# Another load order, blocks and a later root in the first steps of a two-block transformer kernel on one Trainium2 core

## Chip, core and metric

One core of a Trainium2 chip. The metric is the device time of one execution, in microseconds (us). The inputs and outputs are float32 in HBM; the kernel computes 256 tokens of width 2048 through two transformer blocks.

## What is computed

Only the beginning of the first block matters here. In the reference:

```python
h = rmsnorm(x, norm_attn[l])          # x: 256 x 2048
proj = h @ w_in[l]                    # 2048 x 6144, in q, k, v for heads A and heads B
qa = rope(qa.reshape(B, S, A_HEADS, HEAD_DIM), cos_a, sin_a)
ya = dilated_attention(qa, ka, va)
lam = exp(sum(lq[0] * lq[1])) - exp(sum(lq[2] * lq[3])) + lam_init
```

Behind it come a second kind of attention, an output projection and a gated FFN, then a second block with retention, block attention, gates and a convolved FFN, and a last norm. All of it is the same before and after the change.

## The kernel before, in words

**Steps.** All large products are cut into steps, one weight tile of 512 rows by 512 columns (1 MiB) each, numbered t = 0, 1, 2 and on. The three tiles of lead (LEAD) and a ring of four tiles (RING, `w_raw`) set how far the loads run ahead. A float32 product is made of three: ScalarE rounds a tile to `w_hi` (L1377), VectorE subtracts to get `w_lo` (L1906), and TensorE adds hi x hi, lo x hi and hi x lo. A step is 24 matmuls of 128x512: 2 token halves, 4 row blocks, 3 products (`products`, L834). While TensorE works at step t, ScalarE and VectorE run `split(t + LEAD)` and then `pieces(t)`, in program order.

**The transposed x.** `xt` (2048 x 256) comes from HBM in four quarters into `xt_raw`, ScalarE multiplies by the norm's gains into `xt_hi` (L1353), VectorE makes `xt_lo` (L1920). The norm's scale per token is applied later, when results are read from PSUM: for that x itself is loaded too, ScalarE squares and sums it (`square_sum`, L1404), VectorE makes the mean (`variance`), ScalarE takes the root (`root`), VectorE the reciprocal (`inverse`). Two exponentials for lam stand between.

**The first steps.** The first FIRST = 2 tiles are split by blocks of 128 rows; tile 0 is also loaded by blocks (`first_raw`). SyncE (SP) issues: tile 0 in four DMAs, xt quarter 1, tile 1, xt quarter 2, tile 2, xt quarter 3, tile 3, then half of x (two DMAs), tile 4, the other half of x, tile 5, tile 6 and on; from tile 4 it waits for `lo_ready` of the tile whose slot is taken, four before. ScalarE issues xt quarter 0, the gains and the identity. GpSimd issues both rope tables and lambda at once, and after the first step the two masks and the convolution taps. TensorE waits for the identity, does 14 transposes of it (L1160) to warm up, and goes into step 0 (L844 to L846), which waits block by block.

**Round 0** has 12 steps: 0 to 3 give q, 4 to 7 k, 8 to 11 v. What is done with the q of round 0, by program order on each engine:

- t = 0 and 1, ScalarE: the eight squares. t = 2: VectorE `variance(0)`, lambda sums, `inverse(0)`; ScalarE root and exponentials (`start`, L1590 and L2243).
- t = 3, ScalarE: `read_group` of q out of PSUM, scaled (L1582). t = 3, VectorE: rope on q (`rope_step`, L186; L2077 to L2080), which signals `stage_roped`.
- t = 6, TensorE: after the 24 matmuls of step 6 it waits for `stage_roped` and transposes q with eight transposes (`stage_turn`, L900; the step is in `turn_steps`, L178: `return ROUND_T[r] + 6, ROUND_T[r] + 9`), and only then goes on to step 7. t = 9: the same for k.
- t = 4, VectorE, after `pieces(4)`: `s_sums("rounds1")` (L1993 to L2000), sums of blocks of xt that later steps (from t = 12) use. t = 5, ScalarE: `s_hi_piece`.

VectorE's loop, which sets the order that the steps below follow:

```python
for t in range(FFN1_T):
    ...
    split(t + LEAD)
    if not softmax_step(t):
        pieces(t)
    if ROUNDS_1 and t == 4:
        s_sums("rounds1", 0, a_sum_early, sa_sum)
```

Softmax steps begin at t = 13 (L196), so in all steps of interest the split stands before the pieces.

Of the kernel before, what the change touches and what calls it, by code (L numbers as in the profile page):

```python
# [179 lines left out]
def rope_step(r, j):  # L180

    if r in UNIT_ROUNDS and KIND[r] != "R":
        return STEP[("round", r), ("U3" if r in P3_ROUNDS else "P7", "P4")[j]]
    if (r, j) == (4, 1):
        return STEP[("round", r), "P2"]
    return ROUND_T[r] + (5 if (r, j) == (5, 0) else 4 * j + 3)  # L186

# [24 lines left out]

WARM_UP = 14

FIRST = 2
DMA_SCRATCH = 1024
# [12 lines left out]
def plan_weights():  # L229
# [5 lines left out]
    count = [0] * RAW_SLOTS  # L235
    count[0] = -1

# [239 lines left out]
def build(nc, ins, out):  # L477
# [141 lines left out]
    x_loaded = [sem(f"x_loaded{q}") for q in range(Q)]  # L619
    xt_loaded = [sem(f"xt_loaded{q}") for q in range(Q)]  # L620
    first_raw = [sem(f"first_raw{j}") for j in range(C)]
    ident_loaded = sem("ident_loaded")
# [143 lines left out]
    @block.sync  # L766
    def _(sp):
        xr = ins["x"].rearrange("b (a p) d -> p (b a) d", p=P)
        def load_x(q):
            sp.dma_start(x[:, :, q * N:(q + 1) * N], xr[:, :, q * N:(q + 1) * N]).then_inc(x_loaded[q], 16)  # L770

        first = loads[0]
        for j in range(C):
            sp.dma_start(raw_tile(first.slot)[:, j], ins[first.weight][0][bass.ds(first.row + j * P, P), bass.ds(
                first.col, N)]).then_inc(first_raw[j], 16)
        for k, ld in enumerate(loads):
            if k == 0:
                continue
            if k < RING:
                sp.dma_start(xt_raw[:, C * k:C * (k + 1), :], ins["xt"][:, C * k:C * (k + 1), :]).then_inc(xt_loaded[k], 16)  # L780
            if k in (RING, RING + 1):
                load_x(2 * (k - RING))
                load_x(2 * (k - RING) + 1)
            if ld.made is not None:
                sp.wait_ge(sum_ready, sums[ld.made].count)
            elif ld.release >= 0:
                sp.wait_ge(lo_ready, ld.release + 1)
            sp.dma_start(raw_tile(ld.slot), tile_of(ins[ld.weight][0], ld.row, ld.col)).then_inc(
                raw_ready[ld.slot], 16)

        for tok in range(TOK):
            for q in (2, 3):
                cols = slice(q * N, (q + 1) * N)
                sp.wait_ge(out_dve_ready, 2 * tok + q - 1)
                sp.dma_start(orr[tok][:, cols], x[:, tok, cols]).then_inc(stored, 16)
        sp.wait_ge(stored, 16 * Q * TOK)

    @block.gpsimd
    def _(pool):
        def load(dst, src, signal):  # L800
            pool.dma_start(dst, src).then_inc(signal, 16)

        load(rope_a[:], ins["rope_a"], ropes_loaded)
        load(rope_b[:], ins["rope_b"], ropes_loaded)
        load(lq, ins["lambda_qk"].partition_broadcast(P)[:, 0], lam_loaded)
        pool.wait_ge(tile_used, 1)
        load(mask_a[:], ins["mask_a"], tables_loaded)
# [25 lines left out]
    def _(pe):  # L833
        def products(t, parts, first=True, last=True, shared=False, between=None, signal=tile_used):  # L834
# [4 lines left out]
            if t == 0:  # L839
                for j in range(C):  # L840
                    pe.wait_ge(xt_first_lo_done, j + 1)
                    pe.wait_ge(first_lo_ready, j + 1)
                    for bank, hi, lo in parts:
                        nc.tensor.matmul(bank, hi[:, j, :], w_hi[:, 0, j, :], start=j == 0, stop=False)  # L844
                        nc.tensor.matmul(bank, hi[:, j, :], w_lo[:, 0, j, :], start=False, stop=False)
                        end = nc.tensor.matmul(bank, lo[:, j, :], w_hi[:, 0, j, :], start=False, stop=False)  # L846
                end.then_inc(signal, 1)
                return
            for (bank, hi, lo), first in zip(parts, firsts):
                if between is not None and bank is parts[-1][0]:  # L850
# [306 lines left out]

        pe.wait_ge(ident_loaded, 16)
        for _ in range(WARM_UP):
            nc.tensor.transpose(acc[:, 0, 0, 0:P], ident[:, :], ident[:, :])  # L1160

# [188 lines left out]
    def _(act):  # L1350
        def xt_first_hi(c):
            act.wait_ge(xt_loaded[c // C], 16)
            copy(xt_hi[:, c, :], xt_raw[:, c, :], gains[:, G_ATTN1 + c:G_ATTN1 + c + 1]).then_inc(xt_first_hi_done, 1)  # L1353

        def split(t):
            if t >= STEPS:
                return
            if t == 0:
                for j in range(C):
# [3 lines left out]
                        first_hi_ready, 1)  # L1363
                return
            if t in sums:
                act.wait_ge(sum_ready, sums[t].count)
            else:
                act.wait_ge(raw_ready[steps[t].slot], steps[t].count)
            if t < FIRST:
                for j in range(C):  # L1370
                    nc.scalar.activation(w_hi[:, t, j], raw_tile(steps[t].slot)[:, j], ACT.Copy).then_inc(
                        first_hi_ready, 1)
                return
            if t >= RING:
                act.wait_ge(tile_used, t - RING + 1)
            rows = slice(0, 2) if t in sums and sums[t].name == "E5" else slice(0, C)
# [26 lines left out]

        def square_sum(zn, tok, q):  # L1404
            if squares[0]:
                act.wait_ge(sumsq_done, squares[0])
# [167 lines left out]
        def projections(t):  # L1574
            for r in range(8):
                rs = rstd[:, 0, :] if r < 4 else rstd[:, 3, :]
                plain = r not in UNIT_ROUNDS
                for j in range(2):
                    if (plain or KIND[r] == "R") and t == ROUND_T[r] + 4 * j + 3:
                        if 2 * r + j > 0:  # L1580
# [9 lines left out]
        def start(t):  # L1590
            if t in (0, 1):
                for q in (2 * t, 2 * t + 1):
                    act.wait_ge(x_loaded[q], 16)
                    for tok in range(TOK):
                        square_sum(0, tok, q)
            if t == 2:
                root(0)
# [18 lines left out]

        act.dma_start(xt_raw[:, 0:C, :], ins["xt"][:, 0:C, :]).then_inc(xt_loaded[0], 16)
        act.dma_start(gains[:, :], ins["gains"]).then_inc(gains_loaded, 16)
        act.dma_start(ident[:, :], ins["ident"]).then_inc(ident_loaded, 16)
        act.wait_ge(gains_loaded, 16)  # L1620
# [235 lines left out]
    def _(dve):  # L1856
# [29 lines left out]
        def split(t):  # L1886
# [3 lines left out]
            if t >= STEPS:  # L1890
                return
            if t not in sums:
                dve.wait_ge(raw_ready[steps[t].slot], steps[t].count)
            if t < FIRST:
                for j in range(C):
                    if t == 0:
                        xt_first_lo(j)
                    dve.wait_ge(first_hi_ready, C * t + j + 1)
                    nc.vector.tensor_tensor(w_lo[:, t, j], raw_tile(steps[t].slot)[:, j], w_hi[:, t, j].bitcast(F32),
# [343 lines left out]
        def start(t):  # L2243
            if t == 2:
                variance(0)
# [25 lines left out]
        def softmax_step(t):  # L2271
            return any(KIND[r] != "R" and attention_part(r, t) >= 0 for r in range(8))

        dve.wait_ge(gains_loaded, 16)
        for t in range(LEAD):
# [341 lines left out]
```

## Time and profile before

| what | before |
|---|---|
| device time, median of 3 runs | 2482.72 us (2482.7 to 2482.93) |
| time of the profiled execution | 2482.84 us |
| its span in the profile | 2481.0 us |
| TensorE busy | 2463.4 us (99%) |
| VectorE busy | 2105.0 us (85%) |
| ScalarE busy | 1518.1 us (61%) |
| first matmul of step 0 | 12.00 us after the span's start |

The span runs from the first to the last recorded event of the execution; the 1.8 us that the time has over it lie around it. Times of rows are microseconds from the span's start. Busy time of an engine is the union of its instructions.

### The profile page before, as it was taken

To read this page: it belongs to the slowest core of one execution; us is meant where nothing else is said; L and a number is where in the kernel's file an instruction comes from. 1 tells how busy PE (TensorE), PEld (TensorE's weight loads), DVE (VectorE), ACT (ScalarE), POOL (GpSimd) and SP (SyncE) were. 2 spreads that over 40 slices of the span, in tenths; PEclk is the share of its full clock that TensorE was granted. 3 is DMA by queue.
4 is the path that set the end of the run, shared out by engine and by line. 5 is a ranking of instruction groups with operands and counts; after the bars stand their busy time and mean duration, and the time that the engine had idled before them with its cause. 6 is when DMAs were issued, how large, how long until landed. Compare 5 with 4: busy or idle time off the path is not lost.

```text
span 2481.0 us, 28409 instructions
## 1 busy us (share of the span) xinstructions
PE 2463.4 (99%) x11260; PEld 2040.6 (82%) x11260; DVE 2105.0 (85%) x1717; ACT 1518.1 (61%) x1442; POOL 101.8 (4%) x95
## 2 busy tenths in 40 slices
PE   8999999999999999999999999999999999999998
PEld 7888888888888888888888888888888888888887
DVE  6878667899999999879688787877799999999997
ACT  6645555566666666665565565444566667766666
POOL 0000000000000000000000000000000000000000
PEclk9999999999999999999999999999999999999999
DMA  8546446677777777775455556557557777777775
GB/s 305 177 163 204 152 153 207 210 236 237 237 237 237 236 236 239 212 249 189 168 172 184 187 197 219 174 173 241 173 195 239 230 230 231 231 231 230 230 248 159
DMA packets 262580, 524.57 MB, mean 211 GB/s; under 512 B 9088, under 2 KB 9216, under 8 KB 262192
## 3 DMA queue, kind: packets, MB, share of 16 engines
q1 hardware_dynamic: 238688, 474.51, 55.9%
q0 software_dynamic: 22752, 46.55, 10.3%
q8 instruction: 90, 1.47, 0.2%
q10 hardware_dynamic: 1008, 1.68, 0.2%
q14 instruction: 42, 0.34, 0.0%
HBM read 478.67 MB, written 2.10 MB: 194 GB/s over the span
## 4 chain that ended last, share of the span: by engine, by line
PE 97%; DMA 1%; DVE 1%; ACT 0%; SPq 0%; issue 0%; ACTq 0%; DVEq 0%
PE acc L855 23%; PE acc L859 23%; PE acc L857 23%; PE misc L855 6%; PE misc L859 6%; PE misc L857 6%; PE acc L868 1%; PE acc L872 1%; PE acc L870 1%; PE misc L900 1%; DMA w_raw<-in_w_in 1%; PE misc L908 1%; PE misc L868 1%; PE misc L872 1%; PE misc L870 1%; PE misc L991 0%
## 5 line engine op out<-in xcount | busy, mean ns | idle before, releaser
L1906 DVE TENSOR_TENSOR w_lo<-w_raw,w_hi 128x2048 fp32r<-128x2048 f32 x475 | 1065.6, 2254 | 157.0 <-ACT w_hi L1377 155.6
L1377 ACT ACTIVATE w_hi<-w_raw 128x2048 fp32r<-128x2048 f32 x475 | 896.1, 1890 | 337.7 <-PE acc L859 234.5
L855 PE MATMUL acc<-w_hi,xt_hi 128*128 128x512 f32 x1132 | 447.1, 395 | 0.5 <-DVE w_lo L1906 0.4
L859 PE MATMUL acc<-w_hi,xt_lo 128*128 128x512 f32 x1132 | 441.3, 390 | 0.0
L857 PE MATMUL acc<-w_lo,xt_hi 128*128 128x512 f32 x1132 | 440.6, 389 | 0.0
L855 PEld LDWEIGHTS acc<-w_hi,xt_hi 128*128 128x128 f32 x1132 | 212.6, 188 | 45.0 <-issue 1.3
L859 PEld LDWEIGHTS acc<-w_hi,xt_lo 128*128 128x128 f32 x1132 | 212.4, 188 | 44.9
L857 PEld LDWEIGHTS acc<-w_lo,xt_hi 128*128 128x128 f32 x1132 | 212.7, 188 | 42.6
L1906 DVE TENSOR_TENSOR w_lo<-w_raw_more,w_hi 128x2048 fp32r<-128x2048 f32 (+1 forms) x99 | 222.2, 2244 | 29.8 <-ACT w_hi L1377 29.8
L1377 ACT ACTIVATE w_hi<-w_raw_more 128x2048 fp32r<-128x2048 f32 (+1 forms) x99 | 186.4, 1885 | 58.4 <-DVE w_raw_more L1877 15.8
L1881 DVE TENSOR_TENSOR w_raw<-w_raw 128x2048 f32<-128x2048 f32 x80 | 182.9, 2286 | 0.1
L855 PE MATMUL misc<-w_hi,xt_hi 128*128 128x512 f32 x452 | 178.7, 395 | 0.0
L859 PE MATMUL misc<-w_hi,xt_lo 128*128 128x512 f32 x452 | 176.3, 390 | 0.0
L857 PE MATMUL misc<-w_lo,xt_hi 128*128 128x512 f32 x452 | 176.0, 389 | 0.0
L1380 ACT ACTIVATE staged<-acc 128x1024 f32<-128x1024 f32 x80 | 82.4, 1030 | 116.0 <-PE acc L859 116.0
L855 PE MATMUL acc<-w_hi,h_hi 128*128 128x512 f32 x320 | 126.1, 394 | 0.0
L859 PE MATMUL acc<-w_hi,h_lo 128*128 128x512 f32 x320 | 124.9, 390 | 0.0
L857 PE MATMUL acc<-w_lo,h_hi 128*128 128x512 f32 x320 | 124.6, 389 | 0.0
L855 PE MATMUL acc<-w_hi,ht_hi 128*128 128x512 f32 x320 | 124.6, 389 | 0.0
L857 PE MATMUL acc<-w_lo,ht_hi 128*128 128x512 f32 x320 | 124.5, 389 | 0.0
L859 PE MATMUL acc<-w_hi,ht_lo 128*128 128x512 f32 x320 | 124.5, 389 | 0.0
L830 POOL DMA_DIRECT2D x<-staged x40 | 47.6, 1191 | 1290.1 <-ACT staged L1380 1276.0
(386 smaller groups left out, 4180.8 us busy)
## 6 DMA issues: line engine op xcount, KB each, us to landing
w_raw<-in_w_in SPq DMA_DIRECT2D x135, 1024.0 KB, 5.1
w_raw<-in_w_ffn_up SPq DMA_DIRECT2D x61, 1024.0 KB, 6.1
w_raw<-in_w_ffn_down SPq DMA_DIRECT2D x42, 1024.0 KB, 5.8
x<-staged POOLq DMA_DIRECT2D x80, 512.0 KB, 6.4
w_raw<-in_w_out SPq DMA_DIRECT2D x32, 1024.0 KB, 5.2
w_raw<-in_w_gate SPq DMA_DIRECT2D x32, 1024.0 KB, 6.6
w_raw<-in_w_down SPq DMA_DIRECT2D x32, 1024.0 KB, 7.0
w_raw<-in_w_up SPq DMA_DIRECT2D x27, 1024.0 KB, 5.2
```

The source lines that it names most:

```text
L830: pool.dma_start(x[:, :, n * N:(n + 1) * N], staged[k][:], accum_op=ALU.add).then_inc(staged_added[k], 16)
L855: nc.tensor.matmul(bank, hi[:, j, :], w_hi[:, t % RING, j, :], start=first and j == 0, stop=False, skip_group_check=shared)
L857: nc.tensor.matmul(bank, hi[:, j, :], w_lo[:, t % RING, j, :], start=False, stop=False, skip_group_check=shared)
L859: end = nc.tensor.matmul(bank, lo[:, j, :], w_hi[:, t % RING, j, :], start=False, stop=last and j == C - 1, skip_group_check=shared)
L868: nc.tensor.matmul(bank, hi[:, j, :], w_hi[:, t % RING, j0 + j, :], start=new and j == 0, stop=False, skip_group_check=True)
L870: nc.tensor.matmul(bank, hi[:, j, :], w_lo[:, t % RING, j0 + j, :], start=False, stop=False, skip_group_check=True)
L872: end = nc.tensor.matmul(bank, lo[:, j, :], w_hi[:, t % RING, j0 + j, :], start=False, stop=True, skip_group_check=True)
L900: end = nc.tensor.transpose(misc[:, banks[j // 2], (j % 2) * S + tok * P:(j % 2) * S + (tok + 1) * P], src[:, tok, j * P:(j + 1) * P], ide ...
L1377: nc.scalar.activation(w_hi[:, t % RING, rows], raw_tile(steps[t].slot)[:, rows], ACT.Copy).then_inc(hi_ready, 1)
L1380: return nc.scalar.activation(dst, src, func, scale=scale, **kw)
L1881: nc.vector.tensor_tensor(mine, other, mine, ALU.subtract).then_inc(sum_ready, 1)
L1906: nc.vector.tensor_tensor(w_lo[:, t % RING, rows], raw_tile(steps[t].slot)[:, rows], w_hi[:, t % RING, rows].bitcast(F32), ALU.subtract).t ...
```

## The change

In the order of the file:

- rope on the q of round 0 moves from t = 3 to t = 5 on VectorE, and the read of this q from PSUM from t = 3 to t = 5 on ScalarE. The transposition of q on TensorE stays at t = 6, `s_sums` at t = 4.
- 10 warm-up matmuls of 128x128 on a zeroed part of `junk` (a memset on VectorE) take the place of the 14 transposes of the identity. TensorE waits for the identity at step 4 instead.
- FIRST = RING = 4: tiles 0 to 3 are all loaded by blocks of 128 rows (16 DMAs of 256 KB), split by blocks and waited for by blocks.
- SP's order is now: gains, tile 0, xt quarter 1, tile 1, xt quarter 2, tile 2, xt quarter 3, tile 3, tile 4, tile 5, half of x, tile 6, the other half of x, tile 7 and on. ScalarE issues only xt quarter 0, as two halves.
- GpSimd issues the rope tables, lambda and the identity after step 0, the masks and taps after step 4.
- The squares move from t = 0, 1 to t = 3, 4, root, mean, reciprocal and lambda from t = 2 to t = 5.

```diff
-    return ROUND_T[r] + (5 if (r, j) == (5, 0) else 4 * j + 3)
+    return ROUND_T[r] + (5 if (r, j) in ((0, 0), (5, 0)) else 4 * j + 3)
...
-WARM_UP = 14
-
-FIRST = 2
+WARM_UP = 10
+
+FIRST = RING
...
-        first = loads[0]
-        for j in range(C):
-            sp.dma_start(raw_tile(first.slot)[:, j], ins[first.weight][0][bass.ds(first.row + j * P, P), bass.ds(
-                first.col, N)]).then_inc(first_raw[j], 16)
+        sp.dma_start(gains[:, :], ins["gains"]).then_inc(gains_loaded, 16)
         for k, ld in enumerate(loads):
-            if k == 0:
+            if k < FIRST:
+                if k:
+                    sp.dma_start(xt_raw[:, C * k:C * (k + 1), :], ins["xt"][:, C * k:C * (k + 1), :]).then_inc(
+                        xt_loaded[1 + k], 16)
+                for j in range(C):
+                    sp.dma_start(raw_tile(ld.slot)[:, j], ins[ld.weight][0][bass.ds(ld.row + j * P, P), bass.ds(
+                        ld.col, N)]).then_inc(first_raw[C * k + j], 16)
                 continue
...
-            if k in (RING, RING + 1):
-                load_x(2 * (k - RING))
-                load_x(2 * (k - RING) + 1)
+            if k in (RING + 2, RING + 3):
+                load_x(2 * (k - RING - 2))
+                load_x(2 * (k - RING - 2) + 1)
...
+        pool.wait_ge(tile_used, 1)
         load(rope_a[:], ins["rope_a"], ropes_loaded)
         load(rope_b[:], ins["rope_b"], ropes_loaded)
         load(lq, ins["lambda_qk"].partition_broadcast(P)[:, 0], lam_loaded)
-        pool.wait_ge(tile_used, 1)
+        load(ident[:, :], ins["ident"], ident_loaded)
+        pool.wait_ge(tile_used, 5)
         load(mask_a[:], ins["mask_a"], tables_loaded)
...
+            if t == 4:
+                pe.wait_ge(ident_loaded, 16)
...
-        pe.wait_ge(ident_loaded, 16)
+        pe.wait_ge(warm_ready, 1)
         for _ in range(WARM_UP):
-            nc.tensor.transpose(acc[:, 0, 0, 0:P], ident[:, :], ident[:, :])
+            nc.tensor.matmul(acc[:, 0, 0, 0:P], junk[:, 0:P], junk[:, 0:P], start=True, stop=True)
...
+            if t < FIRST:
+                for j in range(C):
+                    act.wait_ge(first_raw[C * t + j], 16)
+                    nc.scalar.activation(w_hi[:, t, j], raw_tile(steps[t].slot)[:, j], ACT.Copy).then_inc(
+                        first_hi_ready, 1)
+                return
...
-                    if (plain or KIND[r] == "R") and t == ROUND_T[r] + 4 * j + 3:
+                    if (plain or KIND[r] == "R") and t == ROUND_T[r] + 4 * j + (5 if (r, j) == (0, 0) else 3):
...
         def start(t):
-            if t in (0, 1):
-                for q in (2 * t, 2 * t + 1):
+            if t in (3, 4):
+                for q in (2 * t - 6, 2 * t - 5):
                     act.wait_ge(x_loaded[q], 16)
                     for tok in range(TOK):
                         square_sum(0, tok, q)
-            if t == 2:
+            if t == 5:
                 root(0)
...
-        act.dma_start(xt_raw[:, 0:C, :], ins["xt"][:, 0:C, :]).then_inc(xt_loaded[0], 16)
-        act.dma_start(gains[:, :], ins["gains"]).then_inc(gains_loaded, 16)
-        act.dma_start(ident[:, :], ins["ident"]).then_inc(ident_loaded, 16)
+        for half in range(2):
+            rows = slice(2 * half, 2 * half + 2)
+            act.dma_start(xt_raw[:, rows, :], ins["xt"][:, rows, :]).then_inc(xt_loaded[half], 16)
...
         def start(t):
-            if t == 2:
+            if t == 5:
                 variance(0)
...
+        nc.vector.memset(junk[:, 0:P], 0.0).then_inc(warm_ready, 1)
         dve.wait_ge(gains_loaded, 16)
```

## Rows read from the trace of the kernel before

**Rows 1.** Page, busy time by engine, and waits of TensorE over the whole span

```profile
PE 2463.4 (99%) x11260; PEld 2040.6 (82%) x11260; DVE 2105.0 (85%) x1717; ACT 1518.1 (61%) x1442; POOL 101.8 (4%) x95
...
PE acc L1160 <- DMA ident<-in_ident: 9.1, 1, 9.1
PE acc L855 <- DVE w_lo L1906: 0.4, 1, 0.4
```

**Rows 2.** Timeline of PE (start us, us): warm-up, steps 0, 1 and 6, transposition, step 7

```profile
9.10 3.25 PE L1160 MATMUL acc<-ident 128*128 128x128 f32 x14 [9.10 <-DMA ident<-in_ident]
12.00 0.78 PE L844 MATMUL acc<-w_hi,xt_hi 128*128 128x512 f32 x1
...
13.86 0.54 PE L845 MATMUL acc<-w_lo,xt_hi 128*128 128x512 f32 x1
14.23 0.40 PE L846 MATMUL acc<-w_hi,xt_lo 128*128 128x512 f32 x1
14.47 0.40 PE L844 MATMUL acc<-w_hi,xt_hi 128*128 128x512 f32 x1
...
18.58 0.39 PE L855 MATMUL acc<-w_hi,xt_hi 128*128 128x512 f32 x1
...
24.02 0.39 PE L855 MATMUL acc<-w_hi,xt_hi 128*128 128x512 f32 x1
...
46.33 0.50 PE L855 MATMUL acc<-w_hi,xt_hi 128*128 128x512 f32 x1 [0.39 <-DVE w_lo L1906]
...
51.93 1.03 PE L900 MATMUL misc<-ident,qk_stage 128*128 128x128 f32 x8
52.73 0.47 PE L855 MATMUL acc<-w_hi,xt_hi 128*128 128x512 f32 x1
```

**Rows 3.** DMA issues in 0 to 3 us: KB each, us to landing

```profile
y<-in_lambda_qk POOLq DMA_DIRECT2D x1, 128.0 KB, 7.7
rope_a<-in_rope_a POOLq DMA_DIRECT2D x1, 64.0 KB, 6.0
ident<-in_ident ACTq DMA_DIRECT2D x1, 64.0 KB, 7.4
...
rope_b<-in_rope_b POOLq DMA_DIRECT2D x1, 32.0 KB, 6.8
```

**Rows 4.** Tile w_raw, blocks 0 and 3 of tile 0 (windows 0.7:1.1, 2.1:2.3)

```profile
DMA to landing us min/median/max: 5.5/5.5/5.5
...
DMA to landing us min/median/max: 8.3/8.3/8.3
```

**Rows 5.** Timeline of ACT and DVE, first block of tile 0

```profile
8.29 0.61 ACT L1362 ACTIVATE w_hi<-w_raw 128x512 fp32r<-128x512 f32 x1
...
8.94 0.69 DVE L1899 TENSOR_TENSOR w_lo<-w_raw,w_hi 128x512 fp32r<-128x512 f32 x1
```

**Rows 6.** Tile w_raw, tile 7: issue on SP and landing (window 26.7:27)

```profile
L788 SPq DMA_DIRECT2D w_raw<-in_w_in x1: 2199/2199/2199, 26.8 to 26.8; - x1
...
DMA to landing us min/median/max: 14.3/14.3/14.3
```

**Rows 7.** Tile w_raw, tile 8: issue on SP and landing (window 34.0:34.3)

```profile
L788 SPq DMA_DIRECT2D w_raw<-in_w_in x1: 367/367/367, 34.0 to 34.0; - x1
...
DMA to landing us min/median/max: 9.7/9.7/9.7
```

**Rows 8.** DMA issues in 18.9 to 20.5 us: KB each, us to landing

```profile
mask_a<-in_mask_a POOLq DMA_DIRECT2D x1, 256.0 KB, 5.7
mult_a<-in_mult_a POOLq DMA_DIRECT2D x1, 256.0 KB, 6.3
taps<-in_taps POOLq DMA_DIRECT2D x1, 176.0 KB, 6.4
```

**Rows 9.** Timeline of ACT, 31 to 46 us: squares, split 5, root, exponentials, read of q

```profile
31.48 0.61 ACT L1407 ACTIVATE junk<-x 128x512 f32<-128x512 f32 x1
...
34.32 0.19 ACT L1407 ACTIVATION_READ_ACCUMULATOR junk<-x 128x1 f32 x1
...
35.71 1.92 ACT L1377 ACTIVATE w_hi<-w_raw 128x2048 fp32r<-128x2048 f32 x1 [1.20 <-DMA w_raw<-in_w_in]
...
41.85 0.20 ACT L1599 ACTIVATE lams<-lams 128x2 f32<-128x2 f32 x1
...
43.76 1.25 ACT L1380 ACTIVATE qk_stage<-acc,rstd 128x512 f32<-128x512 f32 x2
```

**Rows 10.** Timeline of DVE, 37 to 57 us: splits 5 to 8, rope on q, s_sums

```profile
37.73 2.29 DVE L1906 TENSOR_TENSOR w_lo<-w_raw,w_hi 128x2048 fp32r<-128x2048 f32 x1 [3.76 <-ACT w_hi L1377]
...
46.19 0.29 DVE L2077 TENSOR_TENSOR junk<-qk_stage,rope_a 128x128 f32<-128x128 f32 x1
...
47.18 0.43 DVE L2080 TENSOR_TENSOR qk_stage<-qk_stage,junk 128x256 f32<-128x256 f32 x1
47.52 2.28 DVE L1906 TENSOR_TENSOR w_lo<-w_raw,w_hi 128x2048 fp32r<-128x2048 f32 x1
49.72 2.29 DVE L1993 TENSOR_TENSOR a_sum_early<-xt_hi,xt_lo 128x2048 f32<-128x2048 f32 x1
...
54.70 2.28 DVE L1906 TENSOR_TENSOR w_lo<-w_raw,w_hi 128x2048 fp32r<-128x2048 f32 x1
```

**Rows 11.** Stretches (busy PE, PEld, DVE, ACT, POOL; PEclk; DMA; GB/s) and last matmul

```profile
12.00:13.80 1.80, 1.80 (x6) 1.47 (x5) 1.65 (x5) 1.45 (x4) 0.00 (x0) 1.00 1.06 420
...
2472.62 0.39 PE L859 MATMUL acc<-w_hi,h_last_lo 128*128 128x512 f32 x1
...
2473.10:2475.00 1.90, 0.00 (x0) 0.00 (x0) 1.55 (x4) 0.82 (x3) 0.00 (x0) 1.00 0.00 0
2475.00:2475.50 0.50, 0.00 (x0) 0.00 (x0) 0.32 (x2) 0.27 (x2) 0.00 (x0) 0.68 0.00 0
2475.50:2477.00 1.50, 0.00 (x0) 0.00 (x0) 0.99 (x2) 1.18 (x2) 0.00 (x0) 0.50 0.20 74
```

More of the change, by code:

```diff
@@ L235, in plan_weights @@
     count = [0] * RAW_SLOTS
-    count[0] = -1
+    for slot in range(RING):
+        count[slot] = -1
     def load(weight, row, col, release, slots=RING, last_sum=None):
@@ L619, in build @@
     x_loaded = [sem(f"x_loaded{q}") for q in range(Q)]
-    xt_loaded = [sem(f"xt_loaded{q}") for q in range(Q)]
-    first_raw = [sem(f"first_raw{j}") for j in range(C)]
+    xt_loaded = [sem(f"xt_loaded{c}") for c in range(2)] + [sem(f"xt_quarter_loaded{q}") for q in range(1, Q)]
+    first_raw = [sem(f"first_raw{j}") for j in range(C * FIRST)]
+    warm_ready = sem("warm_ready")
     ident_loaded = sem("ident_loaded")
@@ L770, in load_x @@
             sp.dma_start(x[:, :, q * N:(q + 1) * N], xr[:, :, q * N:(q + 1) * N]).then_inc(x_loaded[q], 16)
-        first = loads[0]
-        for j in range(C):
-            sp.dma_start(raw_tile(first.slot)[:, j], ins[first.weight][0][bass.ds(first.row + j * P, P), bass.ds(
-                first.col, N)]).then_inc(first_raw[j], 16)
+        sp.dma_start(gains[:, :], ins["gains"]).then_inc(gains_loaded, 16)
         for k, ld in enumerate(loads):
-            if k == 0:
-                continue
-            if k < RING:
-                sp.dma_start(xt_raw[:, C * k:C * (k + 1), :], ins["xt"][:, C * k:C * (k + 1), :]).then_inc(xt_loaded[k], 16)
-            if k in (RING, RING + 1):
-                load_x(2 * (k - RING))
-                load_x(2 * (k - RING) + 1)
+            if k < FIRST:
[5 more added lines that the diff above has]
+                        ld.col, N)]).then_inc(first_raw[C * k + j], 16)
+                continue
+            if k in (RING + 2, RING + 3):
+                load_x(2 * (k - RING - 2))
+                load_x(2 * (k - RING - 2) + 1)
             if ld.made is not None:
@@ L1351, in xt_first_hi @@
         def xt_first_hi(c):
-            act.wait_ge(xt_loaded[c // C], 16)
+            act.wait_ge(xt_loaded[c // 2 if c < C else 1 + c // C], 16)
             copy(xt_hi[:, c, :], xt_raw[:, c, :], gains[:, G_ATTN1 + c:G_ATTN1 + c + 1]).then_inc(xt_first_hi_done, 1)
@@ L1368, in split @@
                 act.wait_ge(raw_ready[steps[t].slot], steps[t].count)
[L1369 to L1375, printed above, removed]
+            act.wait_ge(tile_used, t - RING + 1)
             rows = slice(0, 2) if t in sums and sums[t].name == "E5" else slice(0, C)
@@ L1404, in square_sum @@
         def square_sum(zn, tok, q):
+            if not squares[0]:
+                act.wait_ge(tile_used, 1)
             if squares[0]:
@@ L1891, in split @@
                 return
-            if t not in sums:
+            if t not in sums and t >= FIRST:
                 dve.wait_ge(raw_ready[steps[t].slot], steps[t].count)
@@ L1897, in split @@
                         xt_first_lo(j)
+                    dve.wait_ge(first_raw[C * t + j], 16)
                     dve.wait_ge(first_hi_ready, C * t + j + 1)
```

## The prediction

> **What bounds the kernel now.** I read the page first: TensorE is busy 2463.4 of 2481.0 us, and in the list of its waits only two entries stand for the whole span, 9.1 us for the identity at the start and 0.4 us for a `w_lo` [rows 1]. So the time is the moment at which TensorE starts, plus its work, plus a short tail; whatever moves TensorE at the start moves the end by as much, if nothing gives it back. TensorE's timeline shows where that moment lies: the warm-up from 9.10, step 0 from 12.00, step 1's first matmul at 18.58 and step 2's at 24.02, so one step is 5.44 us (24 matmuls 0.227 us apart), step 6 from 46.33 after the 0.4 us wait, the transposes of q at 51.93, step 7 at 52.73 [rows 2]. No other step is late. Then I followed what the change moves onto TensorE's path, and there the decisive place is not step 0 but that transposition of q: TensorE doesn't go to step 7 before VectorE has roped q. Before, rope ends at 47.61 (47.18 + 0.43 [rows 10]) and TensorE comes at 51.93: 4.3 us to spare.
>
> **Part 1, the start: a gain of some 3.5 us up to the transposes.** Before, ScalarE's chain hangs on the gains, issued behind xt quarter 0, and its first `w_hi` starts at 8.29; a block then takes from the start of its `w_hi` at 8.29 to the end of its `w_lo` at 9.63, 1.34 us [rows 5], and TensorE could have begun near 9.7 but is in its warm-up until 12.00 [rows 2]. After, gains are first on SP and the warm-up needs no load, so step 0 hangs on the blocks. The last block of tile 0 lands before at 10.4 (issued near 2.1, 8.3 later), the first, issued at 0.7, at 0.7 + 5.5 = 6.2 [rows 4]. The tables taken out of the way (lambda, both ropes, identity: 288 KB, 0.28 MiB [rows 3]) give back 0.28 x 2.7 = 0.76 us (2.7 us per MiB from landings: tile 7 at 26.8 + 14.3 = 41.1, tile 8 at 34.0 + 9.7 = 43.7, which is 2.6 [rows 6, 7]); SP issues one DMA more ahead, some 0.4. So its last block lands near 10.1 and is split by 11.5; the first, landing near 6.2 plus those 0.4, is split by 7.9. The 10 warm-up matmuls, by the 2.9 us of 14 [rows 2] some 2.1 us, start near 1 and end near 3.3; TensorE then stands still for over 4 us, and at the end of the kernel the granted clock falls to 0.68 and then 0.50 from 2.3 us after the last matmul [rows 11]. I therefore take the warm-up to be lost and step 0 to start at half clock (1.2 GHz). Before, TensorE is active from 9.10 until its spacing goes from 0.43 to 0.24 us at 14.2 [rows 2], 5.1 us. With 5.1 us at 0.43 from 7.9 and the rest at 0.227: 12 matmuls by 13.0, 12 more by 15.7. Before, step 1 begins at 18.58 [rows 2]. TensorE is ahead by 2.9 us, 3.3 with the 0.4 us wait of step 6, which goes too: tiles 4 to 6 no longer queue behind x. Later tiles are in time: tile 1 must be split by 16 to 18 and its blocks land some 0.8 us before the 14.4 of before. TensorE would end step 6 at 15.7 + 6 x 5.44 = 48.4 and be at the transposes there, where before it was at 51.93: 3.5 us. Were it warm in step 0, at some 46.
>
> **Part 2, rope on q comes later than TensorE: the gain is gone and more.** At t = 5 VectorE's order is split(8), mean, reciprocal, rope; and t = 4 before it holds split(7) and `s_sums`. Nothing in the diff moves `s_sums` or the transposition at t = 6. So the chain is:
>
> - Tile 7 lands. Before it was 41.1 [rows 6], with tiles 0 to 7, all of xt and x, and the masks and taps (688 KB, 0.67 MiB [rows 8]) in front. Now masks and taps wait for step 4 to end, near 37, so they are almost all behind it: 0.67 x 2.7 = 1.8 us less, 39.3. The move of x behind tiles 4 and 5 changes nothing here: all of x is still ahead of tile 7.
> - `w_hi` and `w_lo` of tile 7: from the landing of tile 5, which ends ScalarE's wait at 35.7, to the end of its `w_lo` at 37.73 + 2.29 = 40.02, 4.3 us [rows 9, 10]. To 43.6. ScalarE is free: tile 6 lands some 6 us ahead of tile 7 (one tile and 1 MiB of x between), near 33.3, its `w_hi` takes 1.9, and the squares of the first half of x, four 0.76 apart from 31.48 to 34.51 [rows 9], end near 38.3.
> - `s_sums` and `w_lo` of tile 8: from the end of `w_lo` 7 (47.52 + 2.28 = 49.80) to that of `w_lo` 8 (54.70 + 2.28 = 56.98), 7.18 us [rows 10]. To 50.8. Tile 8 landed at 43.7 and does so still, and its `w_hi` is ready by 46: hidden under `s_sums`.
> - Mean, root, reciprocal, two table loads, exponentials: from 40.02 to 41.85 + 0.20 = 42.05, 2.03 us [rows 9, 10]. To 52.9.
> - Read of q by ScalarE 1.25 us [rows 9], rope from 46.19 to 47.61, 1.42 us [rows 10], 0.05 between. To 55.6.
>
> TensorE's transposes start at 55.6 instead of 51.93: **3.7 us later**, and it has stood still for 55.6 - 48.4 = 7.2 us. Part 1 then has no say in the time at all: a faster start only lengthens this wait. Masks and taps, the identity (needed at step 4, asked for near 16), the blocks of tiles 1 to 3 and the memset cost nothing, being hidden under this wait; `s_hi_piece`, `s_lo_piece` and rope on k follow by program order with the same or more room than before, as TensorE is later by 3.7 us.
>
> **Part 3, the clock after the wait: some 2.4 us.** The profile shows the clock falling 2.3 us after the last matmul, to the lower of its two levels [rows 11]; 7.2 us is thrice that. How long TensorE then runs at 1.2 GHz only the start shows. Counted from first activity, 5.1 us: 8 transposes take 8 x 0.207 = 1.66 instead of 0.80 us, and 3.4 us of matmuls at 0.43 are 8, each 0.20 too long: 0.86 + 1.6 = 2.5 us. Counted from the first 128x512 matmul, 2.2 us (12.00 to 14.2): 0.86 + 1.0 = 1.9 us. I take 2.4; the bounds are 0 (no fall) and 5 (twice the time at half clock).
>
> **Sum.** +3.7 +2.4 = +6.1 us on the profiled execution's 2482.84 us, which is 0.12 above the median of the runs: **2488.9 us** against the median 2482.72, +0.25%. A measurement of this kernel can tell some 0.2% from no change, that is 5 us.
>
> **Bounds.** Landing of tile 7: before's steady pace starts late (blocks of tile 0 land 1.4 us apart), and with fewer small tables in the way all may shift by up to 1 us earlier; 16 more issues and masks that come before tile 7 may make it 0.8 later. ScalarE's squares hold the chain at 38.3 in any case. So 54.6 to 56.4 for rope. With a clock cost of 1.5 to 3.4: +4.2 to +7.9, its own range 2486.9 to 2490.6.
>
> **Rivals.**
>
> 1. *Faster: rope doesn't hold TensorE back.* Place: the wait of TensorE for `stage_roped` at t = 6. It decides once rope ends before TensorE's step 6 does, 48.4 or earlier, which takes 7 us out of the chain of part 2. For it: rope before had 4.3 us to spare, and the loads' order favours tiles. Against: every link has a measured row and `s_sums` alone is 5 us. Then the start's gain reaches the end: -3.5, 2479.2, or -5.9, 2476.8, if TensorE is warm from step 0. Chance 0.12 (0.08 of it faster by over 0.2%).
> 2. *The clock doesn't fall, or hardly.* +3.7 to +4.7: 2486.4. For it: the start's stretch has a granted clock of 1.00 beside a spacing of 0.43 [rows 2, 11], so the record isn't complete. Against: the fall at the tail. Chance 0.10, within 0.2%.
> 3. *Loads run better than in the sum.* Tile 7 lands 1.5 us or more earlier and the squares too: rope ends by 54, 2485 to 2487. Chance 0.07, within 0.2%.
> 4. *Blocks are slow.* The blocks of tile 0 land 1.4 us apart, a whole tile takes 2.7. If 256 KB blocks took that for themselves, the 12 new ones would cost 12 x (1.4 - 0.7) = 8.4 us on tile 7 and so on rope: 2497. Against: in these rows three queues share the engines. The Trainium skill ("DMA: Bandwidth & Descriptors", bandwidth) has a rule that speaks for it, to batch transfers to 1 MiB or more; no row shows it for queued blocks. Chance 0.07, slower.
>
> The forecast itself has 0.64, of which 0.55 lie above 0.2% (over 2487.7) and 0.09 below. Slower 0.55 + 0.07 = 0.62; within 0.30; faster 0.08. The range 2484.8 to 2491.8 leaves out rival 1 (0.12) and rival 4 (0.07).
>
> **What the profile after would show.** Right: first matmul of step 0 near 7.9; tile 7 landing near 39.3; `s_sums` directly behind `w_lo` 7 and ahead of the mean; TensorE's list of waits with one long entry of 7 to 9 us for rope's line at L900, transposes at 55.6, the granted clock below 1 behind it and spacings of 0.43 us. Wrong: if the L900 entry is absent or TensorE comes to step 7 before 52.7, part 2 fails; if the spacing behind the wait is 0.227 at once, part 3 does; if tile 7 lands after 42, it is rival 4.

## The result, and the profile after the change

The changed kernel takes 2487.54 us (median of 17 runs, 2486.76 to 2488.34) against 2482.8 us (17 runs, 2482.17 to 2483.72) of the kernel before: ratio 1.0019, 95% interval 1.0012 to 1.0026. It is slower by 4.7 us, 0.19%: clear of no change by the interval, and a hair under the 0.2% that the prediction had set for what a measurement can tell. Predicted were 2488.9 us, 2484.8 to 2491.8. In the experiments below, one run of the changed kernel without the later q (2538.91 us) and one of the kernel before beside it (3557.81 us) had a mean granted clock of 0.92 and 0.66 where all others have at least 0.997, and the ratios leave these two out.

| what | before | after |
|---|---|---|
| time of the profiled execution | 2482.84 us | 2488.09 us |
| its span | 2481.0 us | 2486.3 us |
| TensorE busy | 2463.4 us | 2467.5 us |
| first matmul of step 0 | 12.00 us | 7.17 us |
| transposes of q begin | 51.93 us | 54.65 us |
| last matmul begins | 2472.62 us | 2478.41 us |

TensorE's waits over the whole span, after (engine, line waited for: us in total, times, longest; answers to [rows 1]):

```profile
PE misc L907 <- DVE qk_stage L2090: 8.5, 1, 8.5
PE acc L849 <- DVE w_lo L1909: 1.5, 1, 1.5
PE acc L1167 <- DVE junk L2284: 1.1, 1, 1.1
```

The two short ones lie at the start: one ahead of the warm-up, one between it and step 0. The long one is new: TensorE at the transposes of q (L907 of the changed kernel is L900 before), waiting for the last operation of rope. Its timeline, after (start us, us; answers to [rows 2]):

```profile
1.06 4.63 PE L1167 MATMUL acc<-junk 128*128 128x128 f32 x20 [1.06 <-DVE junk L2284]
...
7.17 0.47 PE L849 MATMUL acc<-w_hi,xt_hi 128*128 128x512 f32 x1 [1.48 <-DVE w_lo L1909]
7.47 0.40 PE L850 MATMUL acc<-w_lo,xt_hi 128*128 128x512 f32 x1
...
13.23 0.47 PE L862 MATMUL acc<-w_hi,xt_hi 128*128 128x512 f32 x1
...
54.65 1.97 PE L907 MATMUL misc<-ident,qk_stage 128*128 128x128 f32 x8 [8.50 <-DVE qk_stage L2090]
56.27 0.78 PE L862 MATMUL acc<-w_hi,xt_hi 128*128 128x512 f32 x1
56.84 0.63 PE L864 MATMUL acc<-w_lo,xt_hi 128*128 128x512 f32 x1
57.27 0.63 PE L866 MATMUL acc<-w_hi,xt_lo 128*128 128x512 f32 x1
...
60.68 0.43 PE L864 MATMUL acc<-w_lo,xt_hi 128*128 128x512 f32 x1
60.95 0.39 PE L866 MATMUL acc<-w_hi,xt_lo 128*128 128x512 f32 x1
...
2478.41 0.39 PE L866 MATMUL acc<-w_hi,h_last_lo 128*128 128x512 f32 x1
```

Step 1 begins at 13.23 instead of 18.58, 5.35 us earlier; at the transposes TensorE stands 8.5 us and is 2.72 us later than before; behind them the transposes take 1.62 instead of 0.80 us and the matmuls come 0.43 us apart until 60.68. From the start of the transposes to the last matmul it is 2423.76 us (2478.41 - 54.65) against 2420.69 before: 3.07 us more. Behind the last matmul the span is 0.54 us shorter than before (7.89 against 8.43 us), and all kernels built on the changed one have this shorter end (7.8 to 7.9 us); its cause stays open. So 2.72 + 3.07 - 0.54 = 5.25 us is what the profiled execution lost. The stretches show the clock (busy PE, PEld, DVE, ACT, POOL; PEclk; DMA; GB/s; answers to [rows 11]):

```profile
46.00:54.00 8.00, 0.15 (x1) 0.00 (x0) 5.69 (x14) 4.13 (x7) 0.00 (x0) 0.78 0.77 267
54.65:60.00 5.35, 5.35 (x17) 4.58 (x18) 3.25 (x3) 4.40 (x4) 0.00 (x0) 0.50 0.00 0
60.70:62.00 1.30, 1.30 (x7) 1.09 (x6) 1.30 (x2) 0.00 (x0) 0.00 (x0) 0.97 0.86 291
```

It falls within the wait and stands at half, the lower of its two levels, through the transposes and ten matmuls. VectorE's timeline, after (answers to [rows 10]), gives the reason of the wait:

```profile
40.39 2.29 DVE L1916 TENSOR_TENSOR w_lo<-w_raw,w_hi 128x2048 fp32r<-128x2048 f32 x1 [2.72 <-ACT w_hi L1384]
42.60 2.28 DVE L2003 TENSOR_TENSOR a_sum_early<-xt_hi,xt_lo 128x2048 f32<-128x2048 f32 x1
...
47.58 2.28 DVE L1916 TENSOR_TENSOR w_lo<-w_raw,w_hi 128x2048 fp32r<-128x2048 f32 x1
49.78 0.15 DVE L2047 TENSOR_REDUCE var<-sumsq 128x2 f32<-128x8 f32 x1
...
54.17 0.43 DVE L2090 TENSOR_TENSOR qk_stage<-qk_stage,junk 128x256 f32<-128x256 f32 x1
```

The split of tile 7 ends at 42.68, the block sums follow at once, then the split of tile 8, and only at 49.78 the mean; rope ends at 54.60. ScalarE had all squares done at 43.2 and its table loaded at 46.3, and waited 3.84 us for the mean:

```profile
38.37 1.92 ACT L1384 ACTIVATE w_hi<-w_raw 128x2048 fp32r<-128x2048 f32 x1 [0.57 <-DMA w_raw<-in_w_in]
...
50.18 0.20 ACT L1422 ACTIVATE sd<-var 128x2 f32<-128x2 f32 x1 [3.84 <-DVE var L2053]
```

### The profile page after: what moved, and what is told of

It is laid out like the page before. It is cut to its first block, busy times and chain, and to the rows that moved or that the text cites. A ratio compares the mean times of both kernels' runs of the same rounds, so it can differ in the third digit from the quotient of the medians.

```text
span 2486.3 us, 28462 instructions
## 1 busy us (share of the span) xinstructions
PE 2467.5 (99%) x11266; PEld 2043.6 (82%) x11266; DVE 2106.2 (85%) x1724; ACT 1519.1 (61%) x1448; POOL 102.3 (4%) x96
## 3 DMA queue, kind: packets, MB, share of 16 engines
q0 software_dynamic: 22784, 46.62, 10.2%
q8 instruction: 90, 1.47, 0.2%
## 4 chain that ended last, share of the span: by engine, by line
PE 97%; DVE 1%; DMA 1%; ACT 0%; SPq 0%; issue 0%; DVEq 0%; ACTq 0%
PE acc L862 23%; PE acc L866 23%; PE acc L864 22%; PE misc L862 6%; PE misc L866 6%; PE misc L864 6%; PE acc L879 1%; PE acc L875 1%; PE acc L877 1%; PE misc L907 1%; PE misc L915 1%; PE misc L875 1%; PE misc L879 1%; PE misc L877 1%; DMA w_raw<-in_w_in 1%; PE misc L998 0%
## 5 line engine op out<-in xcount | busy, mean ns | idle before, releaser
L1916 DVE TENSOR_TENSOR w_lo<-w_raw,w_hi 128x2048 fp32r<-128x2048 f32 (+1 forms) x473 | 1061.2, 2254 | 161.2 <-ACT w_hi L1384 159.7
L1384 ACT ACTIVATE w_hi<-w_raw 128x2048 fp32r<-128x2048 f32 (+1 forms) x473 | 892.1, 1890 | 345.7 <-PE acc L866 236.3
L835 POOL DMA_DIRECT2D x<-staged x40 | 47.7, 1191 | 1290.8 <-ACT staged L1387 1276.4
```

What stands on the lines that cost most here:

```text
L835: pool.dma_start(x[:, :, n * N:(n + 1) * N], staged[k][:], accum_op=ALU.add).then_inc(staged_added[k], 16)
L1384: nc.scalar.activation(w_hi[:, t % RING, rows], raw_tile(steps[t].slot)[:, rows], ACT.Copy).then_inc(hi_ready, 1)
L1916: nc.vector.tensor_tensor(w_lo[:, t % RING, rows], raw_tile(steps[t].slot)[:, rows], w_hi[:, t % RING, rows].bitcast(F32), ALU.subtract).t ...
```

## The experiments

Eleven kernels, each against the kernel before on the same chip. In the first four I asked what the wait and the clock are worth.

**Transpose q later.**

```diff
-    return ROUND_T[r] + 6, ROUND_T[r] + 9
+    return ROUND_T[r] + (8 if r == 0 else 6), ROUND_T[r] + 9
```

> The changed kernel with one edit: TensorE transposes the q of round 0 after step 8 instead of after step 6. Theory A (the wait for rope on q, 8.5 us, and the cold clock behind it are the whole loss): rope ends near 54.6 us, TensorE ends step 8 near 57, no wait; what is left is the earlier start, step 1 at 13.23 instead of 18.58 us and no 0.39 us wait at step 6, so 5.7 us under the kernel before: 2477.1. Theory B (the wait is only where a general lateness of tiles or VectorE shows): another wait (for w_lo, or for k's rope after step 9) takes its place and the time stays above 2483.

Measured 2482.74 us (2481.08 to 2483.8), ratio 0.9998 (0.9989 to 1.0007). The 8.5 us wait is gone and with it 4.8 us, but not the 10.4 of theory A: TensorE's waits in the profiled execution (2481.1 us) show what I had overlooked.

```profile
PE acc L862 <- ACT qk_stage L1387: 1.8, 1, 1.8
...
PE misc L907 <- DVE q_t L2241: 0.9, 1, 0.9
PE acc L862 <- DVE w_lo L1916: 0.2, 1, 0.2
```

Step 8 needs the PSUM banks that q stands in, so it waits for ScalarE's read of q, which hangs on the same late root; and k's transposition waits for the copy of q. Behind the 1.8 us wait the clock fell as well:

```profile
51.50:53.20 1.70, 0.00 (x0) 0.00 (x0) 0.31 (x2) 1.69 (x5) 0.00 (x0) 1.00 0.85 287
53.30:57.00 3.70, 3.70 (x10) 2.89 (x11) 1.45 (x5) 3.70 (x3) 0.00 (x0) 0.56 0.33 129
```

The matmuls of this stretch cost 1.6 us more than at full pace. So theory A named one of two consumers of the same late chain.

**Block sums later, q still transposed after step 6.**

```diff
-            if ROUNDS_1 and t == 5:
+            if ROUNDS_1 and t == 7:
                 s_hi_piece("rounds1", sa_hi, sa_sum)
...
-            if ROUNDS_1 and t == 4:
+            if ROUNDS_1 and t == 6:
                 s_sums("rounds1", 0, a_sum_early, sa_sum)
-            if ROUNDS_1 and t == 6:
+            if ROUNDS_1 and t == 8:
                 s_lo_piece("rounds1", sa_lo, sa_hi, sa_sum)
```

> The changed kernel with the block sums of xt (s_sums) moved on VectorE from t = 4 to t = 6, and the rounding of them from t = 5 and 6 to t = 7 and 8; q is still transposed after step 6. Theory A: the chain to rope loses the sums, but tile 8's w_hi (ends at 45.03 us) now holds it, so w_lo of tile 8 ends at 47.3 instead of 49.86 and rope at 52.1; TensorE still waits 5.9 us and the clock still falls: 2.5 us under the changed kernel, 2485.0. Theory B: if the chain were set by loads (tile 8's landing) the sums would have been hidden and nothing changes, 2487.5; if the clock doesn't fall in 5.9 us, 2482.5.

Measured 2485.48 us, ratio 1.0010 (1.0001 to 1.0019): 2.1 us off, 2.5 expected. In its profile the transposes begin at 52.78 behind a wait of 3.93 us, and the clock fell all the same (1.62 us for the transposes, matmuls 0.43 us apart). The sums were in the chain; without them ScalarE's `w_hi` of tile 8 is, for which VectorE now waits:

```profile
52.78 1.97 PE L907 MATMUL misc<-ident,qk_stage 128*128 128x128 f32 x8 [3.93 <-DVE qk_stage L2090]
...
45.72 2.29 DVE L1916 TENSOR_TENSOR w_lo<-w_raw,w_hi 128x2048 fp32r<-128x2048 f32 x1 [2.46 <-ACT w_hi L1384]
```

From the transposes to the last matmul (2475.97) it is 2423.19 us, 2.5 more than before: the price of the clock behind this wait.

**Fill the wait with matmuls.**

```diff
+                    banks_free(("turn", r, j))
+                    for _ in range(70 if n == 0 else 0):
+                        nc.tensor.matmul(misc[:, 0, 0:S], xt_hi[:, 0, 0:P], xt_hi[:, 0, :], start=True, stop=True)
                     pe.wait_ge(stage_roped, n + 1)
-                    banks_free(("turn", r, j))
```

> The changed kernel with 70 extra matmuls of 128x256 on xt_hi (some 0.11 us each, 7.8 us in all) into the free bank just ahead of the wait for rope on q. They do nothing for the output. The wait itself stays, rope ends at the same time, but TensorE is not idle in it. Theory A (2.7 us of the loss are the wait, 2.5 us the clock after it): the transposes take 0.8 instead of 1.6 us, step 7's matmuls come every 0.227 us at once, 2.5 us less: 2485.0. Theory B (the slow matmuls of step 7 come from contention with the splits and DMAs, not from idleness): 2487.5 or more.

Measured 2485.93 us, ratio 1.0013 (1.0004 to 1.0022). TensorE, its transposes, step 7 and the last matmul:

```profile
47.23 8.55 PE L1037 MATMUL misc<-xt_hi 128*128 128x256 f32 x70
55.62 1.04 PE L907 MATMUL misc<-ident,qk_stage 128*128 128x128 f32 x8
56.41 0.47 PE L862 MATMUL acc<-w_hi,xt_hi 128*128 128x512 f32 x1
56.73 0.39 PE L864 MATMUL acc<-w_lo,xt_hi 128*128 128x512 f32 x1
...
2476.33 0.39 PE L866 MATMUL acc<-w_hi,h_last_lo 128*128 128x512 f32 x1
```

The filler ran over, so the transposes begin 0.97 us later than in the changed kernel (55.62 against 54.65), and yet the profiled time is 2.16 us less (2485.93 against 2488.09). The idle wait's after-effect is worth 0.97 + 2.16 = 3.1 us. The last matmul says the same: it begins 2420.71 us behind the transposes (2476.33 - 55.62), as in the kernel before (2420.69), where the changed kernel has 2423.76. By the medians, of which the changed kernel's lies 0.55 us under its profiled execution, it is 2.6 us. The same splits and DMAs are in both kernels, so it is idleness and not contention.

**No warm-up, q transposed after step 8.** Against the run with q after step 8:

```diff
-WARM_UP = 10
+WARM_UP = 0
```

> As the run that transposes q after step 8, but without the 10 warm-up matmuls. It shows what the warm-up of the change is worth where nothing behind it swallows the gain. Theory A: step 0 begins near 7.2 us at half clock and stays so for some 4 to 5 us, of which the waits for blocks hide a part: 1.5 to 2.5 us over the run with the warm-up, some 2479. Theory B (the step is set by the blocks' arrival, the clock doesn't matter): same time as that run, 2477.1.

Measured 2481.93 us (2481.33 to 2483.53), with the warm-up 2482.74 (2481.08 to 2483.8): no loss. Both theories fail in part: step 0 did run at half clock without the warm-up (0.43 us apart until 11.4), but TensorE then only comes later to the waits behind it: 0.41 instead of 1.80 us at step 8 (and no half clock behind it), 2.6 instead of 0.9 at k's transposes, which begin at 68.11 and 67.86. VectorE's copy of q sets that place in both. Behind the 2.6 us the clock falls here, and behind the 0.9 us it doesn't (the same stretch, without and with the warm-up):

```profile
70.00:72.00 2.00, 2.00 (x6) 1.60 (x5) 2.00 (x3) 1.61 (x1) 0.00 (x0) 0.50 0.87 337
...
70.00:72.00 2.00, 2.00 (x11) 1.65 (x10) 2.00 (x2) 1.37 (x1) 0.00 (x0) 1.00 0.79 306
```

That is why the profiled execution without the warm-up takes 2482.91 us and the one with it 2481.1, though k's transposes begin only 0.25 us apart. The runs of both kernels form the same two groups, 2481.08 to 2481.95 and 2482.74 to 2483.8 us (6 and 5 runs without the warm-up, 5 and 6 with it). That the group follows from whether the clock falls once more is inferred from these two profiles; the difference of the medians, 0.8 us, only says which group holds the middle run. So this pair can't price the warm-up; that needs a kernel without those waits.

The next four test the new reading: what costs is that squares, root, read and rope of q as a chain end after TensorE needs them.

**q after step 8, k after step 10, block sums at t = 6.** The two edits above together, and 10 for k.

> The changed kernel with q of round 0 transposed after step 8, its k after step 10 instead of 9, and the block sums at t = 6 (rounding at 7 and 8). Transposing q after step 8 alone left three waits: 1.80 us at step 8 for the read of q out of its bank, behind it 3.4 us at half clock, and 0.91 us at k's transposition for the copy of q on VectorE. Theory A (what costs is that the whole chain squares, root, read, rope of q is later than TensorE; moving one consumer only finds the next): with the sums out of the chain q is read by 51.2 us, before TensorE asks for the bank at 51.3, and all three waits go: 2477 to 2479 (at most 0.5 us for w_lo at step 10), the higher if step 0 runs at half clock. Theory B (the clock falls or tiles are late whatever the order): 2481 or more, as the run with q after step 8.

Measured 2477.77 us, ratio 0.9980 (0.9971 to 0.9989). From step 0 on TensorE's list of waits is empty. The start's gain reaches the end, although in this profile the clock fell within step 0 (half clock from 7.96 to 11.38 us).

**Root, read and rope at t = 4, q transposed after step 7.**

```diff
-    return ROUND_T[r] + 6, ROUND_T[r] + 9
+    return (ROUND_T[r] + 7, ROUND_T[r] + 9) if r == 0 else (ROUND_T[r] + 6, ROUND_T[r] + 9)
...
-            if t == 5:
+            if t == 4:
                 root(0)
...
-            if t == 5:
+            if t == 4:
                 variance(0)
```

and 4 for 5 in `rope_step` and in the read of q; block sums at t = 6.

> The changed kernel with root, read of q and rope on q at t = 4 instead of 5 (squares stay at t = 3 and 4), q transposed after step 7, k after 9, block sums at t = 6. Theory A: root follows w_lo of tile 7 (42.7 us) and the squares (43.1): exponentials by 45.2, q read by 46.5, rope by 48; TensorE wants the bank and the transposition at 51.3: no wait there, perhaps 0.2 at step 8 for w_lo: 2477 to 2479. Theory B: 2481 or more.

Measured 2477.03 us (2476.37 to 2478.25), ratio 0.9977 (0.9967 to 0.9986). VectorE's timeline shows the mean right behind the last square, and rope done at 49.15, before TensorE comes at 51.02 (last line):

```profile
40.57 2.29 DVE L1916 TENSOR_TENSOR w_lo<-w_raw,w_hi 128x2048 fp32r<-128x2048 f32 x1 [2.72 <-ACT w_hi L1384]
43.44 0.16 DVE L2047 TENSOR_REDUCE var<-sumsq 128x2 f32<-128x8 f32 x1 [0.58 <-ACT junk L1416]
...
48.72 0.43 DVE L2090 TENSOR_TENSOR qk_stage<-qk_stage,junk 128x256 f32<-128x256 f32 x1
...
53.92 2.29 DVE L2003 TENSOR_TENSOR a_sum_early<-xt_hi,xt_lo 128x2048 f32<-128x2048 f32 x1
...
51.02 1.03 PE L907 MATMUL misc<-ident,qk_stage 128*128 128x128 f32 x8
```

**The kernel before with only the later q.** Squares at 3 and 4, root, read and rope at 5, all else as before.

> The kernel before with only the last part of the change: squares at t = 3 and 4, root at 5, read of q and rope at 5; loads, blocks and warm-up as before. Theory A: tile 7 lands at 41.1 us as before, w_lo of tile 7 ends at 45.4, of tile 8 at 52.6, rope at 57.4, TensorE comes at 51.5 and waits 5.9 us, and the clock falls: +5.5 from the wait and +2.5 to 3 from the clock: 2491. Theory B (the shift alone is harmless and the new loads make the lateness): 2483 or less.

Measured 2492.72 us, ratio 1.0039 (1.0026 to 1.0052), 5 runs: the shift alone costs 10 us, more than the 8 expected.

```profile
PE misc L900 <- DVE qk_stage L2080: 8.2, 1, 8.2
...
45.40 2.29 DVE L1906 TENSOR_TENSOR w_lo<-w_raw,w_hi 128x2048 fp32r<-128x2048 f32 x1 [2.45 <-ACT w_hi L1377]
```

Rope ends at 59.6, 2.2 us after the 57.4 of the expectation: x comes early there, but its eight squares now stand on ScalarE in front of the `w_hi` of tiles 7 and 8, which I had taken for free, so the split of tile 7 ends at 47.7 instead of 45.4 (its `w_hi` begins at 43.40, at once behind the first four squares).

**The changed kernel without the later q.** Squares at 0 and 1, root at 2, read and rope at 3, x before tiles 4 and 5.

> The changed kernel with the last part undone: squares at t = 0 and 1, root at 2, read of q and rope at 3, x loaded before tiles 4 and 5 as in the kernel before; early tiles by blocks, gains first, later small tables and the new warm-up stay. Theory A: w_lo of tile 5 is late by 2.3 us at step 5 (x is in front of it) and that of tile 6 by another 0.8 us; rope on q is in time. 5.8 us of earlier start less 3.1 us of waits, and up to 2 us more if the clock falls in them: 2480 to 2482. Theory B (the later q is needed to keep any of the gain): 2482.7 or more.

Measured 2480.0 us, ratio 0.9989 (0.9980 to 0.9999). In its profile step 0 ran at half clock until 10.3. The waits are where they were expected, 2.1 us in all instead of 3.1, and the clock didn't fall behind them:

```profile
PE acc L862 <- DVE w_lo L1916: 2.1, 3, 1.5
```

The last three price parts of the start, on the version with root at t = 4. They ran on another chip than that version itself; the kernel before took 2482.59 us on the one and 2482.60 on the other.

**14 warm-up matmuls** (`WARM_UP = 14`).

> The version with root, read and rope at t = 4 (2477.03 us), with 14 warm-up matmuls instead of 10. 10 end at 5.7 us and step 0 can start near 6.9 to 7.5; in some profiles step 0 then ran at full, in others at half clock for up to 5 us. Theory A (the gap decides): 14 end near 7.4 at the latest, no gap, step 0 at full clock in all executions: same median or up to 1 us less (2476.0 to 2477.0). Theory B (the clock of step 0 doesn't reach the end, since tile 1 sets step 1's start): 2477.0 or, for the warm-up that runs over, 0.3 more.

Measured 2476.52 us (2476.33 to 2476.78), ratio 0.9975 (0.9965 to 0.9984). It has the lowest median, and the spread of its runs is 0.45 us against 1.9 with 10. It beats both kernels, by 6.1 us the one before.

**No warm-up** (`WARM_UP = 0`).

> The same version (2477.03 us) without any warm-up. Theory A: step 0 begins at half clock and TensorE, which no longer waits for q, carries it to the end: 1 to 2 us more, 2478 to 2479. Theory B (nothing hangs on the warm-up, as the pair of runs with q after step 8 suggests, 2482.7 and 2481.9): 2477.0.

Measured 2477.36 us (2476.89 to 2478.88): 0.3 us more than with 10 and 0.8 more than with 14. The 0.3 us is within the spread of both (1.9 and 2.0 us). The warm-up is worth less than a microsecond. In the profile step 0 is at half clock until 9.65 and step 1 begins at 13.70, against 12.81 with 10 and 13.37 with 14 warm-up matmuls, where the clock is full and TensorE stands still for a moment between blocks or steps; of the 0.89 us to the version with 10, 0.40 are left at the last matmul.

**Tiles 2 and 3 loaded and split whole** (`FIRST = 2`).

```diff
-FIRST = RING
+FIRST = 2
...
-            if k < FIRST:
+            if k < RING:
                 if k:
                     sp.dma_start(xt_raw[:, C * k:C * (k + 1), :], ins["xt"][:, C * k:C * (k + 1), :]).then_inc(
                         xt_loaded[1 + k], 16)
+            if k < FIRST:
                 for j in range(C):
...
```

Tile 1 is still loaded by blocks, so the expectation's words on tile 1 don't apply.

> The same version (2477.03 us) with FIRST = 2: tiles 1 to 3 are loaded whole as in the kernel before, tile 1 is still split by blocks, tiles 2 and 3 whole. It prices the blocks. Theory A (blocks let the split follow the loads): tile 1 lands near 13.5, its w_hi takes 0.6 and its first w_lo 0.7 more, so step 1 starts at 14.8 instead of 13.1: 1.5 to 2 us more, 2478.5 to 2479. Theory B (rival 4 of the prediction: 256 KB blocks are slow to load): at most 2477 or less.

Measured 2478.9 us, ratio 0.9986 (0.9977 to 0.9995): 1.9 us more, of which the trace ties 1.4 to the whole tiles, as a wait at step 2, whose tile is the first whole one. The rest isn't separated; step 0 ran at half clock in this profile and at full clock in that of the version with blocks.

```profile
PE acc L863 <- DVE w_lo L1918: 1.4, 1, 1.4
```

The blocks help here. That they load slowly (rival 4) is refuted by the landing of tile 7, which is the same without and with tiles 2 and 3 in blocks: 26.0 + 12.6 = 38.6 and 24.9 + 13.6 = 38.5 us.

```profile
L792 SPq DMA_DIRECT2D w_raw<-in_w_in x1: 367/367/367, 26.0 to 26.0; - x1
DMA to landing us min/median/max: 12.6/12.6/12.6
...
L791 SPq DMA_DIRECT2D w_raw<-in_w_in x1: 1844/1844/1844, 24.9 to 24.9; - x1
DMA to landing us min/median/max: 13.6/13.6/13.6
```

## Why the prediction was right, and where its steps were off

**The mechanism held.** The wait for rope at t = 6 took the place of the wait at the start; it is in the profile (8.5 us at L907), taking the block sums out of its chain moved its end by 1.9 us, and taking the whole chain out of TensorE's way brought 10 us. The later q alone, put into the kernel before, costs 10 us.

**Part 2, +3.7 us: measured +2.72.** The chain itself was right to a tenth: from the landing of tile 7 to the end of rope 16.3 us predicted, 54.60 - 38.35 = 16.25 measured. The term that was mis-sized is the landing of tile 7, 39.3 predicted, 38.4 measured:

```profile
L791 SPq DMA_DIRECT2D w_raw<-in_w_in x1: 1302/1302/1302, 24.9 to 24.9; - x1
...
DMA to landing us min/median/max: 13.5/13.5/13.5
```

That lies in the bound I had given (up to 1 us earlier). Why the loads are 0.9 us ahead of the sum was argued (fewer small tables in the first microseconds), and no run separates it.

**Part 3, +2.4 us: measured 3.1.** Both ways of reading the profiled executions give it: the distance from the transposes to the last matmul (3.07 more than before) and the fill experiment (3.1). By the medians it is 2.6. That executions differ in how long the half clock lasts would explain this and the spread of 1.6 us; it was not seen in a second profile.

**The sum.** In the profiled execution the transposes came 1.0 us earlier than forecast, the clock cost 0.7 more, and the end of the span was 0.5 shorter, a term that the sum didn't have: 5.25 instead of 6.1. That the first two pull against each other is luck. The median change is 4.7, since the profiled execution lies 0.55 us above the median of its kernel.

**Part 1 was off, without consequence for the time.** I took the warm-up for 2.1 us and lost. The 10 matmuls on the zeroed tile take 4.63 us, as 20 records of 0.23 us: their price from the 14 transposes, 0.207 each, was the wrong row. They end at 5.69, TensorE stands still for 1.48 us and not for over 4, and in this profile step 0 runs at full clock from 7.17 on (forecast: 7.9, at half clock), so the warm-up was not lost. In the profile with the block sums later the same ten were followed by half clock (until 13.5), as I had assumed; TensorE came to the transposes at 46.15 instead of 48.4 and waited 8.5 instead of 7.2 us. That none of it counts was right for this kernel. The version with root at t = 4 shows what the whole start is worth once nothing swallows it: step 1 begins 5.8 us earlier (12.81 against 18.58), and the median is 5.6 us lower (2477.03 against 2482.59).

**The rivals.** Rival 1 needed the chain to be shorter by 7 us; it wasn't. Its numbers, 2479.2 and 2476.8, are about what the repaired versions reach (2477.8, 2477.0). Rival 2 is refuted by the stretches and by the fill. Rival 3 came half true: tile 7 landed 0.9 us earlier, and a rope at 54.6 is close to the 54 at which it would have counted. Rival 4 is refuted.

**What I missed**, and only the first experiment showed: the transposition is not the only place where TensorE waits for the root. The read of q frees the banks of step 8.

## What to carry to other kernels

When work is moved later to make room for an earlier start, list every engine's order from the move to the next point at which the bound engine waits for it, and add the rows up: a chain that ends late can cost more than the whole start brings (here 10 against 5.6 us), and an unmoved operation that now stands in it is part of that (the block sums, 2.1 us). If a wait goes away and another takes its place, look for the second consumer of the same late value before changing the first. A wait of TensorE is priced as its length plus the half-clock stretch that may follow: here 1.8 us of waiting cost another 1.6, 3.9 us another 2.5, and 8.5 us another 3.1; behind waits of 1.47 us and less no half clock followed.

## What the runs showed of the hardware

The times of rise and fall are those of the clock records in the traces.

- The clock can fall after a wait shorter than the 2.3 us of the tail, and when TensorE is already at work again. With q after step 8 TensorE waited 1.80 us, began again at 53.25 and was at half clock from 53.76 to 57.17; without the warm-up there it waited 2.55 us at k's transposes, began again at 68.11 and was at half clock from 69.41 to 72.82. Behind waits of 0.91 (q after step 8), 1.40 (tiles 2 and 3 whole) and 1.47 us (changed kernel without the later q) no fall is recorded.
- In long waits the fall has no fixed delay: 2.2 us after the last matmul's end with the block sums later (51.09), 3.3 with only the later q (54.79), 4.4 in the changed kernel (50.53).
- Ten warm-up matmuls end at 5.69 in seven of the eight profiles that have them, and the length of the gap behind them doesn't decide the pace of step 0: it was full after 1.25, 1.48 and 1.74 us and half after 1.20, 1.29, 1.98 and 2.19. In the first three the clock rose between 5.97 and 6.41, after the warm-up and before step 0; in the other four it had not risen when step 0 began, and rose between 10.2 and 13.5. What decides between the two isn't shown.
- With 14 warm-up matmuls the clock rose within the warm-up, at 4.64, and step 0 was at full pace in the one profile taken. The same 0.4 us with 14 and with 10 (root at t = 4), seven warm-up records against four:

```profile
4.80:5.20 0.40, 0.40 (x7) 0.40 (x5) 0.38 (x1) 0.00 (x0) 0.00 (x0) 1.00 0.99 328
...
4.80:5.20 0.40, 0.40 (x4) 0.40 (x3) 0.40 (x1) 0.00 (x0) 0.00 (x0) 1.00 1.07 384
```

- A rise within the warm-up didn't protect step 0 from a long gap: with q after step 8, k after step 10 and the sums later it rose at 4.55, the gap was 2.29 us, and the clock fell at 7.96, 0.5 us into step 0.
- How long TensorE works before the pace rises differs: 6.0 us behind the 8.5 us wait (54.65 to 60.68), 5.1 us at the start of the kernel before, 2.8 us without any warm-up (6.83 to 9.65).
